# Long convolution by spectra: the signal's transform one pass ahead, the product of the spectra in four parts

## The chip, the cores and the metric

One core of one Trainium2 chip runs the whole program, in fp32. The metric is the device time of one execution in microseconds, the median of several.

## What is computed

The program is a chain of network blocks: an attention block, a Hyena block, two blocks with mixtures of experts. Only one stage of the Hyena block matters here, its long convolutions (`k_f` is the spectrum of a filter that a small network makes from the inputs, divided by the sum of its absolute values):

```python
def long_conv(u, k_f, skip):
    L = u.shape[1]
    y = jnp.fft.irfft(jnp.fft.rfft(uf, n=2 * L, axis=1) * k_f, n=2 * L, axis=1)[:, :L]
    return (y + uf * skip)
...
z = parts[0]
for o in range(HY_ORDER):                        # 2 orders
    z = parts[o + 1] * long_conv(z, k_f[:, o], skip[o])
```

L is 1024 and there are 1024 channels, so two orders of 1024 channels are convolved.

## The kernel before

`stage_long_conv` works in eight passes (PASSES), each of 256 channels (CCH) of one order; passes 0 to 3 are order 0, passes 4 to 7 order 1. Transforms are matmuls with constant matrices of cosines and sines, split by the token's remainder modulo four (PH = 4 phases, banks `x_bank0` to `x_bank3`) and two tiles of frequencies (MT = 2, index `ft`). One pass j needs, in the order of the data:

- **filters(j)**: TensorE makes eight filter tiles (matmul with `hid` and `w3`, L1861), and VectorE multiplies each with a decay into `filt` (L1998). The eight tiles share the four banks, so the second four wait until the first four are taken out.
- **sizes, totals, norm**: ScalarE takes absolute values into `mag` (two buffers, L1952), VectorE the maximum of the two halves into `total` (L2014), TensorE sums over partitions into `n_bank` (L1901). **tap(j)** on VectorE (L2022, L2024) adds the skip to the filter's first tap. `inverse_size` and `keep_size` (L2031, L2035) make `rnorm`, by which the result is scaled.
- **k_transform(j)**: 48 matmuls (96 records in the trace) on `filt`; ScalarE copies the banks to `xk` (L1958), VectorE's **k_butterfly** (L2042, L2043 and `turn`, L1819 to L1823) makes the spectrum `vk`.
- **the signal's transform**: 32 matmuls (64 records) on `u`; ScalarE copies to `xu`, then VectorE works on each `ft`: two sums and differences (L2067, L2068) and a `turn`; the product with `vk` (L2072 to L2074); its combination (L2075 to L2079); a second `turn` into `z` (L1819 to L1823). In the change these four parts are called enter, multiply, combine and leave.
- **back**: TensorE multiplies `z` with `inv` into two banks, one phase r after the other (16 records each, L1867 on `lc_y_bank`; here Y0 to Y3). VectorE scales each bank by `rnorm` into `y` (L2096; here y0 to y3), GpSimd multiplies `y` into `part` (L2113), and SP stores it.

`passes` runs a prologue, then a loop of six bodies (i = 0 to 5, `more` and `ahead` true), then body(6, more only) and body(7). Each engine runs its own instructions in order and waits on semaphores. Body i on TensorE before: signal i, k_transform(i + 1), the first four filter tiles of pass i + 2, then the wait for `z` of pass i, Y0, the second four tiles, Y1, Y2, norm(i + 2), Y3. VectorE: all parts of the product for both `ft`, the eight filter tiles of i + 2, then y0, two totals, y1, two totals, k_butterfly(i + 1, 0), y2, k_butterfly(i + 1, 1), tap(i + 2), y3, `rnorm` and size.

## Time and profile before

| | us |
|---|---|
| median of 3 runs | 4913.47 (4912.9 to 4920.15) |
| the profiled execution | 4910.12 |
| its span | 4908.1 |
| the long convolution in it | 1873.6 to 2453.8, about 580 |

The span is the time from the first to the last instruction. A row of the trace gives the start and the length in us of an instruction, or of several like ones in a row, its engine and line, the tiles it writes and reads, and how long its engine sat idle before it. PE is TensorE (its matmuls), PEld its weight loads, DVE VectorE, ACT ScalarE, POOL GpSimd. An fp32 matmul makes two records. Successive instructions of one engine overlap a little at their ends, so a chain is added up from start to start.

### The profile page before, as it was taken

The page shows a single profiled execution, that of the slowest core. Times are in us where ns is not written, and L with a number is a line of the kernel's source. Part 1 is how long each engine was busy: PE and PEld are TensorE (multiplying, and loading weights), DVE is VectorE, ACT ScalarE, POOL GpSimd, SP SyncE. Part 2 cuts the span into 40 slices and gives each one's busy share as a digit, 9 for nine tenths or more (in the row PEclk, how much of TensorE's full clock was granted, in tenths as well). Part 3 has the DMA queues.
Part 4 walks back from the last instruction along what each step waited for, and adds up shares of the span by engine and source line. Part 5 has one row for each costly group of instructions (what it writes and reads, how often), then busy time and mean ns, then how long its engine had stood idle before and what let it go on. Part 6 is the DMA issues. An engine that isn't in the chain of part 4 may idle for free. (4 is left out here: it accounts for less than half of the span.)

```text
span 4908.1 us, 59293 instructions
## 1 busy us (share of the span) xinstructions
PE 4173.6 (85%) x20947; PEld 2139.3 (44%) x20947; DVE 1898.4 (39%) x2965; ACT 1097.4 (22%) x1816; POOL 258.2 (5%) x366
## 2 busy tenths in 40 slices
PE   3699699998999998999679997786999599949995
PEld 0355355555444445777534444442333244413331
DVE  1233345443322113898734936532111333321112
ACT  0122255443110012222111135310000234100000
POOL 0000000000000000110100000000000200000001
PEclk7799899999999998999889999997999799969998
DMA  7322221112365511111161112135865511266666
GB/s 258 117 68 63 60 49 38 37 36 84 139 218 210 200 64 56 42 39 52 43 211 35 43 54 102 53 104 232 321 264 214 187 31 49 100 265 228 251 235 261
DMA packets 260939, 627.18 MB, mean 128 GB/s; under 512 B 73549, under 2 KB 153501, under 8 KB 240969
## 3 DMA queue, kind: packets, MB, share of 16 engines
q1 hardware_dynamic: 221906, 508.13, 29.3%
q0 software_dynamic: 19424, 94.01, 5.1%
q10 hardware_dynamic: 19480, 23.31, 1.3%
q8 instruction: 82, 1.34, 0.1%
q14 instruction: 47, 0.39, 0.0%
HBM read 1298.29 MB, written 113.53 MB: 288 GB/s over the span
## 5 line engine op out<-in xcount | busy, mean ns | idle before, releaser
L1645 PE MATMUL hyp_acc<-hy_hT,hyp_early_weights 128*128 128x512 f32 x768 | 335.9, 596 | 0.0
L3423 PE MATMUL blocks_h<-moe_w,blocks_xT 128*32 128x512 f32 x2560 | 291.1, 607 | 42.3 <-issue 42.3
L3423 PE MATMUL blocks_h<-od_hT,blocks_xT 128*32 128x512 f32 x1280 | 290.9, 608 | 25.7 <-DMA moe_w1b<-in_ex_w 20.6
L3444 PE MATMUL blocks_acc<-moe_w,blocks_hidT 128*32 128x512 f32 x2560 | 284.5, 596 | 11.2 <-DMA moe_w<-in_ex_w 9.9
L3423 PE MATMUL blocks_h<-moe_w1b,blocks_xT 128*32 128x512 f32 x1280 | 290.8, 608 | 0.0
L970 PE MATMUL att_scores<-att_kT,att_qT 64*128 64x512 f32 (+3 forms) x768 | 252.2, 549 | 22.7 <-DMA att_v<-scratch_V 22.7
L700 PE MATMUL lat_acc<-lat_w_in,lat_hT 128*128 128x512 f32 (+1 forms) x640 | 244.6, 538 | 2.2 <-DMA lat_w_in<-in_attn_w_in 2.2
L2209 PE MATMUL evp_acc<-ev_hT,evp_early_weights 128*128 128x512 f32 x512 | 224.6, 600 | 7.6 <-DVE evp_qkT L2350 5.6
L906 DVE TENSOR_REDUCE att_nmax<-att_scores 128x1 f32<-128x1280 f32 x128 | 190.2, 1486 | 102.2 <-PE att_scores L970 102.2
L994 PE MATMUL att_turn<-ident,att_probs 128*128 128x128 f32 x1280 | 192.5, 281 | 42.3 <-DVE att_o L936 22.5
L1645 PEld LDWEIGHTS hyp_acc<-hy_hT,hyp_early_weights 128*128 128x128 f32 x768 | 145.1, 191 | 174.3 <-issue 174.2
L874 ACT ACTIVATE att_probs<-att_scores,att_nmax 128x1280 f32<-128x1280 f32 x128 | 169.9, 1327 | 175.2 <-DVE att_nmax L906 172.4
L994 PEld LDWEIGHTS att_turn<-ident,att_probs 128*128 128x128 f32 x1280 | 143.0, 145 | 99.3 <-ACT att_probsT L885 43.8
L1867 PE MATMUL lc_y_bank<-lc_z,lc_inv 128*128 128x256 f32 x512 | 129.9, 416 | 63.5 <-DVE lc_z L1823 63.5
L3423 PEld LDWEIGHTS blocks_h<-moe_w,blocks_xT 128*32 128x32 f32 x2560 | 83.7, 112 | 220.2 <-issue 216.5
L885 ACT ACTIVATE att_probsT<-att_turn 128x512 f32<-128x512 f32 x256 | 139.2, 594 | 162.7 <-PE att_turn L994 162.2
L3423 PEld LDWEIGHTS blocks_h<-od_hT,blocks_xT 128*32 128x32 f32 x1280 | 76.6, 112 | 223.8 <-issue 223.8
L970 PEld LDWEIGHTS att_scores<-att_kT,att_qT 64*128 64x128 f32 (+1 forms) x768 | 113.1, 192 | 128.0 <-issue 127.9
L1867 PE MATMUL lc_x_bank<-lc_filt,lc_early_fwd 128*128 128x256 f32 x768 | 167.1, 379 | 1.3 <-issue 1.3
L700 PEld LDWEIGHTS lat_acc<-lat_w_in,lat_hT 128*128 128x128 f32 x640 | 114.6, 192 | 115.9 <-issue 115.6
L3444 PEld LDWEIGHTS blocks_acc<-moe_w,blocks_hidT 128*32 128x32 f32 x2560 | 79.7, 110 | 185.9 <-issue 180.0
L1004 PE MATMUL att_scores<-att_probsT,att_v 128*64 128x256 f32 x1280 | 152.3, 384 | 6.9 <-DVE att_probsT L915 6.1
(520 smaller groups left out, 6067.5 us busy)
## 6 DMA issues: line engine op xcount, KB each, us to landing
moe_w<-in_ex_w SPq DMA_DIRECT2D x320, 2048.0 KB
od_hT<-in_ex_w SPq DMA_DIRECT2D x80, 2048.0 KB
moe_w1b<-in_ex_w SPq DMA_DIRECT2D x80, 2048.0 KB
hyp_m_weights<-in_mod_w POOLq DMA_DIRECT2D x6, 8192.0 KB, 24.2
mod_weights<-in_ada_w SPq DMA_DIRECT2D x6, 4096.0 KB, 22.7
scratch_y_rows<-blocks_x ACTq DMA_DIRECT2D x40, 512.0 KB, 8.9
hyp_early_weights<-in_hy_w_in SPq DMA_DIRECT2D x8, 2048.0 KB
scratch_parts<-hyp_uT SPq DMA_DIRECT2D x24, 512.0 KB, 3.7
```

Of the source, the lines that this page charges most:

```text
L700: mm = nc.tensor.matmul(acc[:, (s * NCH + c) % 2, 0:b - a], hT[:, s, kt, :], w_in[:, kt, a:b], start=(kt == 0), stop=(kt == KT - 1))
L874: nc.scalar.activation(probs[:, j % 2, :], scores[:, j % 2, 0:KEYS], ACT.Exp, bias=nmax[:, j % 2:j % 2 + 1], accum_out=total[:, j % 2:j % ...
L885: nc.scalar.activation(probsT[:, c % 2, k:k + m, u * P:(u + 1) * P], turn[:, bank("probs", j, g), 0:m, :], ACT.Copy).then_inc(pT_act, 1)
L906: nc.vector.tensor_reduce(nmax[:, j % 2:j % 2 + 1], scores[:, j % 2, 0:KEYS], AX.X, ALU.max, negate=True).then_inc(maxed, 1)
L970: return nc.tensor.matmul(scores[:, b, a:z], qT[e, s, cols], kT[e, s, a:z], start=True, stop=True)
L994: last = nc.tensor.transpose(turn[:, bank("probs", j, g), a, :], probs[:, j % 2, (k + a) * P:(k + a + 1) * P], ident[:, :])
L1004: mm = nc.tensor.matmul(scores[e, 0, SPARE], v[:, 2 * c // TT, kt, :], probsT[:, c % 2, kt, :], start=(kt < 2), stop=(kt >= KTL - 2))
L1645: mm = nc.tensor.matmul(acc[:, m % 2, half * NC:(half + 1) * NC], weights[:, ws, kt, c:c + P], hT[:, kt, half * NC:(half + 1) * NC], start ...
L1867: mm = nc.tensor.matmul(out, m, x, start=(n == 0), stop=(n == len(terms) - 1))
L2209: mm = nc.tensor.matmul(out, lhs(kt), rhs(kt), start=(kt == 0), stop=(kt == KT - 1))
L3423: mm = nc.tensor.matmul(out[mine, :], xT[:, kt, mine], w[l][:, kt, :], start=(kt == 0), stop=(kt == KT - 1))
L3444: mm = nc.tensor.matmul(acc[mine, c, :], hidT[:, kt, mine], w2[l][:, kt, c * NC:(c + 1) * NC], start=(kt == 0), stop=(kt == FT - 1))
```

## The change

Pass i + 1's signal transform, `u_transform(i + 1)`, now stands in body i, behind k_transform(i + 1) and the first four filter tiles of i + 2. It writes the same four banks as the filter tiles, so TensorE first waits until VectorE has taken these four out (`tiles_gone`). The second four tiles come behind the signal's transform and ahead of Y0. The prologue gets the signal of pass 0, and the last body has no transform.

VectorE's product becomes `spectra(i, ft, parts)` with the four parts; `work` takes the place of the in-place `xu`, and `ktmp` lies in `tmp`. For `ft` 0 of pass i + 1, enter and multiply stand in body i between the two butterflies and the second four filter tiles, combine between y0 and y1, leave at the start of body i + 1. `ft` 1 is done whole in its own body. The two butterflies move from between y1 and y3 to ahead of the second four filter tiles, behind the first four. Where the filter work has ended (body 6), leave of `ft` 0 and enter of `ft` 1 of pass 7 stand between y1 and y3, the rest behind y3; body 7 has only the way back, and its product for pass 7 goes into `filt`. The skip is loaded by the pass, one small DMA each.

```diff
-        tmp, ktmp = sb("tmp", [P, PH, 2, CCH]), sb("ktmp", [P, 2, 2, CCH])
+        tmp, work = sb("tmp", [P, PH, 2, CCH]), sb("work", [P, PH, 2, CCH])
+        ktmp = tmp[:, 0:2, :, :]
...
-                sp.dma_start(skip[:, :], skips).then_inc(skip_in, 16)
+                def load_skip(j):
+                    sp.wait_ge(tapped, signals(j))
+                    sp.dma_start(skip[:, :], skips[:, bass.ds(j * CCH, CCH)]).then_inc(skip_in, 16)
...
+                load_skip(1)
...
+                    if ahead:
+                        load_skip(i + 2)
...
-                        if t < PH:
-                            if not isinstance(j, int) or j:
-                                pe.wait_ge(x_copied[b], signals(j * COPIES - MT))
-                        else:
+                        if not isinstance(j, int) or j:
+                            pe.wait_ge(x_copied[b], signals(j * COPIES - (MT if t < PH else 0)))
+                        if t >= PH:
                             pe.wait_ge(filt_ready, signals(j * NF + (t - PH + 1)))
...
+                def u_transform(j):
+                    pe.wait_ge(u_in, signals(j * 16 + 16))
+                    transform(u_parts, lambda ft: u_copied(j, ft) - 1, u_made)
+
+                def tiles_gone(j):
+                    for b in range(PH):
+                        pe.wait_ge(filt_ready, signals(j * NF + (b + 1)))
...
-                    filters(1, range(NF))
+                    filters(1, range(PH))
+                    tiles_gone(1)
+                    u_transform(0)
+                    filters(1, range(PH, NF))
                     norm(1)
                 def body(i, more, ahead):
                     if more:
                         pe.wait_ge(filt_ready, signals(i * NF + 2 * NF))
-                    pe.wait_ge(u_in, signals(i * 16 + 16))
-                    transform(u_parts, lambda ft: u_copied(i, ft) - 1, u_made)
-                    if more:
                         k_transform(i + 1)
                     if ahead:
                         filters(i + 2, range(PH))
+                        tiles_gone(i + 2)
+                    if more:
+                        u_transform(i + 1)
+                    if ahead:
+                        filters(i + 2, range(PH, NF))
                     pe.wait_ge(z_made, signals(i * MT + MT))
                     for r in range(PH):
-                        if ahead and r == 1:
-                            filters(i + 2, range(PH, NF))
                         if ahead and r == PH - 1:
                             norm(i + 2)
                         pe.wait_ge(y_scaled[r % 2], signals(i * (PH // 2) + r // 2))
...
                         for t in range(MT):
                             last = gather(y_bank[r % 2][:, t, :], [
-                                (inv[:, ft, r, cs, t * P:(t + 1) * P], z[:, ft, r, cs, :])
+                                (inv[:, ft, r, cs, t * P:(t + 1) * P], product_of(i)[:, ft, r, cs, :])
...
                 def copies(n, made, dst):
                     for ft in range(MT):
+                        if made is u_made and not (isinstance(n, int) and n == 0):
+                            act.wait_ge(xu_read, signals(n * MT + (ft + 1 - MT)))
...
                     decays(1)
+                    copies(0, u_made, xu)
...
-                    act.wait_ge(z_made, signals(i * MT))
-                    copies(i, u_made, xu)
                     if more:
                         k_copies(i + 1)
                     if ahead:
                         decays(i + 2)
+                    if more:
+                        copies(i + 1, u_made, xu)
+                    if ahead:
                         sizes(i + 2)
...
-                    dve.wait_ge(skip_in, signals(16))
-                    tt(extra[:, :], n_bank[0:1, 0:CCH], skip[:, bass.ds(j * CCH, CCH)], ALU.mult).then_inc(extra_made, 1)
+                    dve.wait_ge(skip_in, signals(j * 16 + 16))
+                    tt(extra[:, :], n_bank[0:1, 0:CCH], skip[:, :], ALU.mult).then_inc(extra_made, 1)
...
-                    dve.wait_ge(z_made, signals(j * MT))
+                    if not (isinstance(j, int) and j == 0):
+                        dve.wait_ge(z_made, signals((j - 1) * MT + (ft + 1)))
...
+                def spectra(i, ft, parts):
+
+
+                    links = Chain(dve, u_steps, i * (MT * U_STEPS) + ft * U_STEPS)
+                    x, k, w = xu[:, ft, :, :, :], vk[:, ft, :, :, :], work[:, :, :, :]
+
+                    def enter():
+                        dve.wait_ge(x_copied[PH - 1], signals(u_copied(i, ft)))
+                        dve.wait_ge(vk_ready, signals(i * MT + MT))
+                        dve.wait_ge(z_made, signals(i * MT + ft))
+                        tt(tmp[:, 0:2, :, :], x[:, 0:2, :, :], x[:, 2:4, :, :], ALU.add)
+                        tt(tmp[:, 2:4, :, :], x[:, 0:2, :, :], x[:, 2:4, :, :], ALU.subtract).then_inc(xu_read, 1)
+                        dve.wait_ge(xu_read, signals(i * MT + (ft + 1)))
+                        links.link(turn(nc.vector, tmp[:, 0, :, :], tmp[:, 1, :, :], tmp[:, 2, :, :], tmp[:, 3, :, :], w, 1))
+
+                    def multiply():
+                        links.n = 1
+                        links.link(tt(tmp[:, :, :, :], w, k, ALU.mult))
+                        tt(w[:, :, 0, :], w[:, :, 0, :], k[:, :, 1, :], ALU.mult)
+                        links.link(tt(w[:, :, 1, :], w[:, :, 1, :], k[:, :, 0, :], ALU.mult))
+
+                    def combine():
+                        links.n = 3
+                        links.link(tt(tmp[:, :, 0, :], tmp[:, :, 0, :], tmp[:, :, 1, :], ALU.subtract))
+                        links.link(tt(tmp[:, :, 1, :], w[:, :, 0, :], w[:, :, 1, :], ALU.add))
+                        tt(w[:, 0:2, :, :], tmp[:, 0:2, :, :], tmp[:, 2:4, :, :], ALU.add)
+                        links.link(tt(w[:, 2:4, :, :], tmp[:, 0:2, :, :], tmp[:, 2:4, :, :], ALU.subtract))
+
+                    def leave():
+                        if product_of(i) is z:
+                            dve.wait_ge(y_made, signals(i * PH))
+                        turn(nc.vector, w[:, 0, :, :], w[:, 1, :, :], w[:, 2, :, :], w[:, 3, :, :],
+                             product_of(i)[:, ft, :, :, :], 3).then_inc(z_made, 1)
+
+                    for part in parts:
+                        (enter, multiply, combine, leave)[part]()
...
-                    filters(1, range(NF))
+                    filters(1, range(PH))
+                    filters(1, range(PH, NF))
+                    spectra(0, 0, range(3))
                     totals(1, range(SUMS))
                     tap(1)
                     inverse_size(0)
...
                 def body(i, more, ahead):
-                    for ft in range(MT):
-                        link = Chain(dve, u_steps, i * (MT * U_STEPS) + ft * U_STEPS).link
-                        x, k = xu[:, ft, :, :, :], vk[:, ft, :, :, :]
-                        dve.wait_ge(x_copied[PH - 1], signals(u_copied(i, ft)))
-
-                        tt(tmp[:, 0:2, :, :], x[:, 0:2, :, :], x[:, 2:4, :, :], ALU.add)
-                        link(tt(tmp[:, 2:4, :, :], x[:, 0:2, :, :], x[:, 2:4, :, :], ALU.subtract))
-                        link(turn(nc.vector, tmp[:, 0, :, :], tmp[:, 1, :, :], tmp[:, 2, :, :], tmp[:, 3, :, :], x, 1))
...
-                        dve.wait_ge(vk_ready, signals(i * MT + (ft + 1)))
-                        link(tt(tmp[:, :, :, :], x, k, ALU.mult))
-                        tt(x[:, :, 0, :], x[:, :, 0, :], k[:, :, 1, :], ALU.mult)
...
-                        tt(x[:, 0:2, :, :], tmp[:, 0:2, :, :], tmp[:, 2:4, :, :], ALU.add)
-                        link(tt(x[:, 2:4, :, :], tmp[:, 0:2, :, :], tmp[:, 2:4, :, :], ALU.subtract))
-                        dve.wait_ge(y_made, signals(i * PH))
-                        turn(nc.vector, x[:, 0, :, :], x[:, 1, :, :], x[:, 2, :, :], x[:, 3, :, :], z[:, ft, :, :, :], 3)\
-                            .then_inc(z_made, 1)
+                    last = isinstance(i, int) and i == PASSES - 1
+                    if not last:
+                        spectra(i, 0, [3])
+                        spectra(i, 1, range(4))
                     if ahead:
                         filters(i + 2, range(PH))
+                    if more:
+                        for ft in range(MT):
+                            k_butterfly(i + 1, ft)
+                        spectra(i + 1, 0, range(2))
+                    if ahead:
                         filters(i + 2, range(PH, NF))
                     dve.wait_ge(rn_made, signals(i + 1))
                     for r in range(PH):
+                        if more and r == 1:
+                            spectra(i + 1, 0, [2])
+                        if more and not ahead:
+                            if r == 2:
+                                spectra(i + 1, 0, [3])
+                            if r == 3:
+                                spectra(i + 1, 1, [0])
                         if ahead and 0 < r <= 2:
                             totals(i + 2, range((r - 1) * PH // 2, r * PH // 2))
-                        if more and r >= PH - MT:
-                            k_butterfly(i + 1, r - (PH - MT))
                         if ahead and r == PH - 1:
                             tap(i + 2)
                         dve.wait_ge(y_made, signals(i * PH + (r + 1)))
                         dve.wait_ge(conv_done, signals(i * PH + max(r - 1, 0)))
                         tt(y[:, r % 2, :, :], y_bank[r % 2][:, :, :], rnorm[:, :].unsqueeze(1).to_broadcast([P, MT, CCH]),
                            ALU.mult).then_inc(y_scaled[r % 2], 1)
+                    if more and not ahead:
+                        spectra(i + 1, 1, range(1, 4))
                     if more:
                         inverse_size(i + 1)
                     if ahead:
```

The order in which TensorE's instructions stand, in the loop's body. Before (L1861 is a filter tile, L1867 every other matmul; counts are matmuls):

```order
L1867 MATMUL lc_x_bank<-lc_u,lc_early_fwd 128x256 x16
...
L1867 MATMUL lc_x_bank<-lc_filt,lc_early_fwd 128x256 x24
...
L1861 MATMUL lc_x_bank<-lc_early_w,lc_early_hid 128x512 x4
...
L1867 MATMUL lc_y_bank<-lc_z,lc_inv 128x256 x8
...
L1861 MATMUL lc_x_bank<-lc_early_w,lc_early_hid 128x512
...
L1867 MATMUL lc_n_bank<-lc_total,lc_early_ones 128x256 x8
L1867 MATMUL lc_y_bank<-lc_z,lc_inv 128x256 x8
```

and in the changed kernel (L1874 and L1880 are the same two lines):

```order
L1880 MATMUL lc_x_bank<-lc_filt,lc_early_fwd 128x256 x24
...
L1874 MATMUL lc_x_bank<-lc_early_w,lc_early_hid 128x512 x4
...
L1880 MATMUL lc_x_bank<-lc_u,lc_early_fwd 128x256 x16
...
L1874 MATMUL lc_x_bank<-lc_early_w,lc_early_hid 128x512 x4
...
L1880 MATMUL lc_y_bank<-lc_z,lc_inv 128x256 x16
...
L1880 MATMUL lc_n_bank<-lc_total,lc_early_ones 128x256 x8
L1880 MATMUL lc_y_bank<-lc_z,lc_inv 128x256 x8
```

The signal's matmuls moved from the head of the body to between the two groups of filter tiles, and nothing stands any more between Y0 and Y1.

VectorE around y0 and y1 in the loop's body. Before:

```order
L1998 TENSOR_TENSOR lc_filt<-lc_x_bank,lc_decay 128x512
...
L2096 TENSOR_TENSOR lc_y<-lc_y_bank,lc_rnorm 128x512
...
L2014 TENSOR_TENSOR lc_total<-lc_mag 128x512
...
L2042 TENSOR_TENSOR lc_ktmp<-lc_xk 128x512
L2043 TENSOR_TENSOR lc_ktmp<-lc_xk 128x512
```

and in the changed kernel (L2094 to L2096 are multiply, L2100 to L2103 combine, L2042 the totals, L2157 the y of one phase):

```order
L2094 TENSOR_TENSOR lc_tmp<-lc_work,lc_vk 128x2048
...
L2026 TENSOR_TENSOR lc_filt<-lc_x_bank,lc_decay 128x512
...
L2157 TENSOR_TENSOR lc_y<-lc_y_bank,lc_rnorm 128x512
L2100 TENSOR_TENSOR lc_tmp<-lc_tmp 128x4x256
...
L2101 TENSOR_TENSOR lc_tmp<-lc_work 128x4x256
...
L2102 TENSOR_TENSOR lc_work<-lc_tmp 128x1024
L2103 TENSOR_TENSOR lc_work<-lc_tmp 128x1024
...
L2042 TENSOR_TENSOR lc_total<-lc_mag 128x512
```

Four long instructions of the next pass's product now stand between y0 and the totals, and the butterflies that stood behind the totals are ahead of the second four filter tiles.

## Rows read from the trace of the kernel before

**Rows 1.** Who TensorE waited for, whole stage: sum, times, longest wait.

```profile
PE lc_y_bank L1867 <- DVE lc_z L1823: 63.5, 8, 28.4
```

**Rows 2.** One pass: stretch, length, busy PE, PEld, DVE, ACT, POOL, PEclk, DMA.

```profile
2072.80:2138.20 65.40, 60.82 (x259) 49.99 (x258) 59.34 (x83) 16.97 (x28) 6.82 (x4) 0.97 0.14 50
```

**Rows 3.** Timeline of TensorE in pass 1: start, length, engine, line, tiles, count.

```profile
2007.90 13.98 PE L1867 MATMUL lc_x_bank<-lc_u,lc_early_fwd 128*128 128x256 f32 x64
...
2021.71 20.88 PE L1867 MATMUL lc_x_bank<-lc_filt,lc_early_fwd 128*128 128x256 f32 x96
...
2042.43 3.60 PE L1861 MATMUL lc_x_bank<-lc_early_w,lc_early_hid 65*128 x8
...
2050.62 5.30 PE L1867 MATMUL lc_y_bank<-lc_z,lc_inv 128*128 128x256 f32 x16 [4.58 <-DVE lc_z L1823]
...
2066.10 3.62 PE L1867 MATMUL lc_n_bank<-lc_total,lc_early_ones 128*128 128x256 f32 x16
```

**Rows 4.** Timeline of VectorE, same pass: first instruction of each part of the product.

```profile
2015.64 1.22 DVE L2067 TENSOR_TENSOR lc_tmp<-lc_xu 128x1024 f32<-128x1024 f32 x1 [1.63 <-ACT lc_xu L1958]
...
2020.80 2.29 DVE L2072 TENSOR_TENSOR lc_tmp<-lc_xu,lc_vk 128x2048 f32<-128x2048 f32 x1
...
2025.52 1.23 DVE L2075 TENSOR_TENSOR lc_tmp<-lc_tmp 128x1024 f32<-128x1024 f32 x1
...
2030.52 0.69 DVE L1819 TENSOR_TENSOR lc_z<-lc_xu 128x512 f32<-128x512 f32 x1
...
2033.07 1.22 DVE L2067 TENSOR_TENSOR lc_tmp<-lc_xu 128x1024 f32<-128x1024 f32 x1
...
2050.41 0.68 DVE L1998 TENSOR_TENSOR lc_filt<-lc_x_bank,lc_decay 128x512 f32<-128x512 f32 x1
...
2051.98 1.87 DVE L1998 TENSOR_TENSOR lc_filt<-lc_x_bank,lc_decay 128x512 f32<-128x512 f32 x3
```

**Rows 5.** Timeline, same pass, from the totals behind y0: VectorE and GpSimd.

```profile
2060.60 2.37 DVE L2014 TENSOR_TENSOR lc_total<-lc_mag 128x512 f32<-128x512 f32 x2
...
2065.76 0.68 DVE L2042 TENSOR_TENSOR lc_ktmp<-lc_xk 128x512 f32<-128x512 f32 x1
...
2069.63 0.68 DVE L2096 TENSOR_TENSOR lc_y<-lc_y_bank,lc_rnorm 128x512 f32<-128x512 f32 x1
...
2070.39 2.25 POOL L2113 TENSOR_TENSOR lc_part<-lc_y,lc_part 128x512 f32<-128x512 f32 x1 [5.10 <-DVE lc_y L2096]
...
2071.55 1.65 DVE L1819 TENSOR_TENSOR lc_vk<-lc_ktmp,lc_xk 128x512 f32<-128x512 f32 x1
```

**Rows 6.** Timeline of VectorE, end of pass 0: y3, reciprocal, size.

```profile
2010.98 0.67 DVE L2096 TENSOR_TENSOR lc_y<-lc_y_bank,lc_rnorm 128x512 f32<-128x512 f32 x1
...
2011.79 1.75 DVE L2031 RECIPROCAL lc_rnorm<-lc_size 128x256 f32<-128x256 f32 x1
...
2013.58 0.42 DVE L2035 COPY lc_size<-lc_n_bank 128x256 f32<-128x256 f32 x1
```

**Rows 7.** Timeline of the stage's prologue: totals, norm, k_transform(0), second filter tiles of pass 1.

```profile
1888.29 1.28 DVE L2014 TENSOR_TENSOR lc_total<-lc_mag 128x512 f32<-128x512 f32 x2
...
1891.85 6.17 PE L1867 MATMUL lc_n_bank<-lc_total,lc_early_ones 128*128 128x256 f32 x16 [4.20 <-DVE lc_total L2014]
...
1899.28 20.96 PE L1867 MATMUL lc_x_bank<-lc_filt,lc_early_fwd 128*128 128x256 f32 x96 [1.26 <-issue]
...
1926.49 6.17 PE L1861 MATMUL lc_x_bank<-lc_early_w,lc_early_hid 65*128 65x512 f32 x8 [2.81 <-DVE lc_filt L2007]
```

**Rows 8.** Timeline of VectorE: y0 of passes 0, 6 and 7.

```profile
1994.89 0.68 DVE L2096 TENSOR_TENSOR lc_y<-lc_y_bank,lc_rnorm 128x512 f32<-128x512 f32 x1
...
2383.32 0.69 DVE L2096 TENSOR_TENSOR lc_y<-lc_y_bank,lc_rnorm 128x512 f32<-128x512 f32 x1 [5.82 <-issue]
...
2441.45 0.69 DVE L2096 TENSOR_TENSOR lc_y<-lc_y_bank,lc_rnorm 128x512 f32<-128x512 f32 x1 [5.72 <-issue]
```

**Rows 9.** DMA issues of the stage: tiles, queue, count, size, us to landing.

```profile
lc_u<-scratch_parts SPq DMA_DIRECT2D x8, 1024.0 KB, 4.8
```

More of the change, by code:

```diff
@@ L1760, in stage_long_conv @@
         inv = sb("inv", [P, MT, PH, 2, MT * P])
-        skip, skip_in = sb("skip", [1, PASSES * CCH]), sem("skip_in")
+        skip = sb("skip", [1, CCH])
         decay, mag = sb("decay", [P, TILES, CCH]), sb("mag", [P, 2, 2, 2, CCH])
@@ L1780, in stage_long_conv @@
                              "extra_made", "tapped"))
-        sized = sem("sized")
+        sized, skip_in, xu_read = sem("sized"), sem("skip_in"), sem("xu_read")
         u_steps, k_steps, vk_ready, z_made, y_made = (
@@ L1788, in stage_long_conv, with product_of @@
         COPIES = 2 * MT
-        U_STEPS = 7
+        U_STEPS = 6
         FIX = 2
         skips = d["hy_skip"].rearrange("a o c -> a (o c)")
+        z_last = filt[:, :, :, :].rearrange("p (m r) v c -> p m r v c", r=PH)
+        def product_of(i):
+            return z_last if isinstance(i, int) and i == PASSES - 1 else z
         def tokens(plane):
@@ L1833, in load_u @@
                     sp.dma_start(tiled(u), tokens(i)).then_inc(u_in, 16)
-                sp.dma_start(skip[:, :], skips).then_inc(skip_in, 16)
+                def load_skip(j):
+                    sp.wait_ge(tapped, signals(j))
+                    sp.dma_start(skip[:, :], skips[:, bass.ds(j * CCH, CCH)]).then_inc(skip_in, 16)
+                load_skip(0)
                 load_u(0)
@@ L2061, in body @@
                 def body(i, more, ahead):
-                    for ft in range(MT):
-                        link = Chain(dve, u_steps, i * (MT * U_STEPS) + ft * U_STEPS).link
-                        x, k = xu[:, ft, :, :, :], vk[:, ft, :, :, :]
-                        dve.wait_ge(x_copied[PH - 1], signals(u_copied(i, ft)))
-                        tt(tmp[:, 0:2, :, :], x[:, 0:2, :, :], x[:, 2:4, :, :], ALU.add)
-                        link(tt(tmp[:, 2:4, :, :], x[:, 0:2, :, :], x[:, 2:4, :, :], ALU.subtract))
-                        link(turn(nc.vector, tmp[:, 0, :, :], tmp[:, 1, :, :], tmp[:, 2, :, :], tmp[:, 3, :, :], x, 1))
-                        dve.wait_ge(vk_ready, signals(i * MT + (ft + 1)))
-                        link(tt(tmp[:, :, :, :], x, k, ALU.mult))
-                        tt(x[:, :, 0, :], x[:, :, 0, :], k[:, :, 1, :], ALU.mult)
-                        link(tt(x[:, :, 1, :], x[:, :, 1, :], k[:, :, 0, :], ALU.mult))
-                        link(tt(tmp[:, :, 0, :], tmp[:, :, 0, :], tmp[:, :, 1, :], ALU.subtract))
-                        link(tt(tmp[:, :, 1, :], x[:, :, 0, :], x[:, :, 1, :], ALU.add))
-                        tt(x[:, 0:2, :, :], tmp[:, 0:2, :, :], tmp[:, 2:4, :, :], ALU.add)
-                        link(tt(x[:, 2:4, :, :], tmp[:, 0:2, :, :], tmp[:, 2:4, :, :], ALU.subtract))
-                        dve.wait_ge(y_made, signals(i * PH))
-                        turn(nc.vector, x[:, 0, :, :], x[:, 1, :, :], x[:, 2, :, :], x[:, 3, :, :], z[:, ft, :, :, :], 3)\
-                            .then_inc(z_made, 1)
+                    last = isinstance(i, int) and i == PASSES - 1
+                    if not last:
+                        spectra(i, 0, [3])
+                        spectra(i, 1, range(4))
                     if ahead:
                         filters(i + 2, range(PH))
+                    if more:
[3 more added lines that the diff above has]
+                    if ahead:
                         filters(i + 2, range(PH, NF))
```

## The prediction

> **What bounds the kernel now.** The change lies in one stage, so I read only that. First, who waited for whom: in the whole stage TensorE waited for data only for the product `z` on VectorE, 63.5 us in eight waits, the longest 28.4 [rows 1]. Second, one pass: of 65.4 us TensorE is busy 60.8, VectorE 59.3, the granted clock is 0.97 of full [rows 2]. Two engines are nearly full; the reader should see that emptying one wait soon meets the other. Third, TensorE's timeline [rows 3]. A full-speed record takes 20.72 / 96 = 0.216 us (start of the 96 records at 2021.71 to the next row). So a pass needs 13.8 (signal, 64) + 20.7 (filter spectrum, 96) + 2 x 3.4 (filter tiles) + 4 x 3.45 (Y0 to Y3) + 3.45 (norm) = 58.6 us. The rest of 65.4 is one stall of about 5 us in front of Y0 and its sequel: Y0 takes 5.30 where 16 like records take 3.62, because the PE clock, granted 2.4 GHz before, is at 1.2 GHz after the stall.
>
> **What the change removes.** The product `z` of a pass is now finished about 20 us into the body, while TensorE still has 38 us of transforms to do. The wait in front of Y0 goes: at most 65.4 - 58.6 = 6.8 us a pass. At the end of the stage there is more: between y0 of pass 6 and y0 of pass 7 lie 58.1 us [rows 8], most of it the whole product of pass 7 with TensorE idle.
>
> **The VectorE chain.** I cut VectorE's work by starts [rows 4]: enter 2015.64 to 2020.80 = 5.16; multiply 4.72; combine 5.00; leave 2.55; all four 17.43. Four filter tiles with the first-tap repair 2050.41 to 2053.85 = 3.44, so four further ones 4 x 0.61 = 2.44. A butterfly 2065.76 to 2069.63 = 3.87 [rows 5]. y3 to the reciprocal 0.81, then 1.79, then the copy's 0.4: 3.0 [rows 6]. A y takes 0.61 to the next start. Two totals take 1.28 alone [rows 7] but 2.37 behind a y [rows 5]: GpSimd's multiply starts then. Behind y2 it is a `turn` instruction that takes 1.65 where 0.69 is usual, while GpSimd's takes 2.25. So each y that is followed by work on VectorE costs about 1.05 more.
>
> The page "SBUF — State Buffer" of the Trainium skill (section "Who interferes with whom") says that a VectorE instruction with two SBUF inputs and a GpSimd instruction that reads SBUF exclude each other, the later one waiting to the end. The trace agrees in kind; taken literally, with GpSimd's undisturbed length for the hold, it would make each case some 0.2 us dearer. The rule speaks against this change, since combine is such work. The sum uses the 1.05 of the rows.
>
> **A pass of the loop, from y0.** y0 0.6, combine 5.0 + 1.05, two totals 1.2, y1 0.6, a wait of 0.4 for ScalarE's second absolute value, two totals 1.2 + 1.05: 11.1 us until the last total. Only then may norm run; Y2 was done long before, 6.9 us behind Y0. So a new stall of about 4 us stands in front of norm. It resembles the removed one (5 us), so I give it a like sequel. Its bounds are the 1.7 that Y0 lost in the shown pass [rows 3] and the 2.55 that a norm lost in the prologue (6.17 against 3.62) [rows 7, 3], below them nothing; I take 2.0, near the loop's own row. Norm 3.45, Y3 3.45, 2.0, handovers 0.4: y3 starts at 20.4, Y3 ended at 20.2, and there TensorE starts the next filter spectrum.
>
> From y3 VectorE goes 3.0 + leave 2.55 + the whole `ft` 1, 17.43, + four filter tiles 3.44 = 26.4. TensorE has done 20.7 + 3.4 = 24.1 by then and stands at `tiles_gone` until 26.6 after its start: a second stall of 2.5 us behind filter tiles. The nearest row is the prologue's 2.81 us stall, also behind four filter tiles: the eight records behind it take 6.17 where 3.60 is usual [rows 7, 3], so the clock was down. I charge 1.5 (ends: 0 and 2.6). Then the signal 13.8 + 1.5 to 42.0, filter tiles to 45.4, Y0 to 49.1. VectorE is at 26.6 + two butterflies 7.7 + enter and multiply 9.9 + four tiles 2.4 = 46.7, and waits for Y0. From y0 to y0: 20.2 + 49.1 = **69.3 us**.
>
> **The last passes.** Pass 5 to 6 has no filter work in its second half and VectorE carries it: 20.4 + 3.0 + 2.55 + 17.43 + 7.74 + 9.88 = 61.0. Before, the six intervals from y0 of pass 0 to y0 of pass 6 took 2383.32 - 1994.89 = 388.4 [rows 8]. Now 5 x 69.3 + 61.0 = 407.5: **+19.1**. Pass 6 to 7: four y 2.4, combine 5.0, leave 2.55, enter 5.16, then multiply, combine and leave 12.3, four GpSimd holds 4.2, together 31.6, then Y0 of pass 7 at 1.2 GHz 5.6 (3.62 + 2.0) and handovers: 37.4 instead of 58.1: **-20.7**. Behind y0 of pass 7 nothing changes.
>
> **The prologue pays for the pass that is ahead.** Up to k_transform(0), which starts at 1899.28 and lasts 20.7 [rows 7], nothing changes. Its filter tiles come out of the banks at about 1928.3 (the second ones could start at 1926.49 on the first being out, three more at 0.61). TensorE has then stood for 5 us, so signal 0 runs 13.8 + 2.0 to 1944.2; second filter tiles out at 1948.3; enter, multiply, combine 14.9 to 1963.2; totals 3.6 and norm with tap 7.4 (1888.29 to 1891.85 to 1899.28) to 1974.2, the start of k_transform(1). By the scheme above, here without the first tail, y0 of pass 0 comes 48.1 later: 2022.3 against 1994.89: **+27.4**.
>
> What costs nothing: `tmp` shared with the butterflies, since VectorE runs both in order. The signal's load is issued behind the store and the reload of `part` on SP; three transfers of 1 MB at 4.8 each [rows 9] are 14.4 us, and the data is wanted 26.7 us into the body. The skip loads wait for a tap of the pass before and hold SP for nothing; the small row is wanted 60 us later. The other bound, if SP came late, would be a stall as long as it is late; no row suggests it.
>
> **Sum.** 27.4 + 19.1 - 20.7 = +25.8 us. On the profiled execution's 4910.12 that is 4935.9; that execution lies 3.35 below the median of 4913.47, so for the median I forecast **4939 us**. About 0.2% (10 us) is what this kernel's measurement can tell from no change.
>
> **Rivals.** (a) *The clock stays up.* The stalls are shorter than the removed one, and a stall of 4 us between full matmuls has no row here. Then an interval is 65.8, the six take 5 x 65.8 + 59.0 = 388.0, and the prologue 25.9, the tail -20.7: +4.8, or about 4918. The intermediate, one stall with a cold sequel, gives 5 x 1.5 to 2.0 more, 4926 to 4929, and still counts as mine. (b) *It ends faster: GpSimd does not hold combine.* Place: behind y0 and y1, in front of norm. If combine and the totals run undisturbed, the stall before norm shrinks from 4 to 2 us, an interval is 63.7 with the clock up, the six take 5 x 63.7 + 57 = 375.5, the last 33: 25.9 - 12.9 - 25 = -12, 4901. It decides from an interval of about 63.5 to 64 on: there the eight passes balance the prologue. For it: an interval below 64 leaves 5 us of idle or slow TensorE, which the old one had too. Against it: three of four y in the old trace show the hold. (c) *Worse:* both stalls leave TensorE slow for longer, as the upper bounds of 2.6 each allow, and the loop's back edge on VectorE, hidden by a wait before, becomes visible: 2 to 3 us a pass, 4950 to 4955. (d) *It does not do what it says:* `z` still late. Excluded nearly: its last part is 23 us into a body in which Y0 cannot start before 41.
>
> **Chances.** Mine with the intermediate 0.58 (4925 to 4948), (c) 0.16, (a) 0.15, (b) 0.09, (d) 0.02. Faster by over 0.2%: 0.08; within 0.2%: 0.13; slower: 0.79. For 8 in 10 the range takes in (a)'s time and (c)'s: 4913 to 4958.
>
> **What the changed profile would show.** TensorE's wait for `z` only once with weight, at pass 7, some 20 us; new waits for `lc_total` of about 4 us before norm and for `lc_filt` of 2.5 us before the signal; y0 of pass 0 near 2022; intervals near 69; the last one near 37; instructions behind y0 and y1 longer by 1. My forecast is wrong if intervals are under 66, if the granted clock in the loop is not below the old 0.97, or if the first y0 comes before 2015.

## The result, and the profile after

The changed kernel takes 4947.35 us against 4914.01 us before (medians of four runs each): a ratio of 1.0066, 95% interval 1.0046 to 1.0085. It is slower, as forecast, and 4947 lies inside the range of 4913 to 4958; the forecast was 4939. A second series, beside other kernels below, gave 1.0054 (1.0042 to 1.0066), 26.9 us.

The profiled execution took 4957.55 us, 47.4 more than the profiled one of before. Of that, 2.8 us lie ahead of the long convolution (it starts at 1876.43, not 1873.65), 31.1 in it (609.2 us from the first filter matmul to the start of the last y, before 578.1), and 13.5 behind it, where nothing was changed. In the second series' profile the stage is 605.8 us, 27.7 longer than before, about the 26.9 measured there, and the rest of that execution is 6.0 us longer than in the profiled one of before. So only the stage is explained here.

TensorE in a pass of the loop of the changed kernel, to be held against [rows 3] (start, length, engine, line, tiles, count, idle before it and its releaser):

```profile
2137.23 3.60 PE L1874 MATMUL lc_x_bank<-lc_early_w,lc_early_hid 65*128 x8
2143.40 15.48 PE L1880 MATMUL lc_x_bank<-lc_u,lc_early_fwd 128*128 128x256 f32 x64 [2.57 <-DVE lc_filt L2026]
2158.72 3.60 PE L1874 MATMUL lc_x_bank<-lc_early_w,lc_early_hid 65*128 x8
2162.15 10.53 PE L1880 MATMUL lc_y_bank<-lc_z,lc_inv 128*128 128x256 f32 x48
2176.68 5.41 PE L1880 MATMUL lc_n_bank<-lc_total,lc_early_ones 128*128 128x256 f32 x16 [4.00 <-DVE lc_total L2042]
2181.92 3.62 PE L1880 MATMUL lc_y_bank<-lc_z,lc_inv 128*128 128x256 f32 x16
```

The stall in front of Y0 is gone, and Y0 to Y2 run through at full speed. Two stalls stand in its place: 2.57 us until VectorE has taken the filter tiles out, and 4.00 us until the last total. Behind each, TensorE is slow: the signal's transform takes 15.48 where it took 13.98, norm 5.41 where it took 3.62. The next pass is worse in both:

```profile
2212.26 3.35 PE L1880 MATMUL lc_x_bank<-lc_u,lc_early_fwd 128*128 128x256 f32 x7 [2.57 <-DVE lc_filt L2026]
...
2228.97 3.60 PE L1874 MATMUL lc_x_bank<-lc_early_w,lc_early_hid 65*128 x8
...
2246.93 6.25 PE L1880 MATMUL lc_n_bank<-lc_total,lc_early_ones 128*128 128x256 f32 x16 [3.99 <-DVE lc_total L2042]
```

There the signal lasts from 2212.26 to 2228.97, and norm 6.25. Who waited for whom in the stage (engine and line, what it waited for, sum, times, longest), against [rows 1]:

```profile
PE lc_n_bank L1880 <- DVE lc_total L2042: 47.1, 8, 18.9
PE lc_y_bank L1880 <- DVE lc_filt L1830: 20.3, 1, 20.3
PE lc_x_bank L1880 <- DVE lc_filt L2026: 19.2, 7, 4.9
```

The 63.5 us of waits for the product have become 20.3, and TensorE's waits for totals and tiles, 11.2 us before and all of them in the prologue, have become 66.3. VectorE and GpSimd behind y0 of pass 0, against [rows 5]:

```profile
2025.81 0.69 DVE L2157 TENSOR_TENSOR lc_y<-lc_y_bank,lc_rnorm 128x512 f32<-128x512 f32 x1 [0.75 <-PE lc_y_bank L1880]
2026.42 1.22 DVE L2100 TENSOR_TENSOR lc_tmp<-lc_tmp 128x1024 f32<-128x1024 f32 x1
2026.59 2.17 POOL L2176 TENSOR_TENSOR lc_part<-lc_y,lc_part 128x512 f32<-128x512 f32 x1 [259.39 <-DVE lc_y L2157]
2027.67 2.17 DVE L2101 TENSOR_TENSOR lc_tmp<-lc_work 128x1024 f32<-128x1024 f32 x1
...
2035.21 1.42 DVE L2042 TENSOR_TENSOR lc_total<-lc_mag 128x512 f32<-128x512 f32 x1 [0.25 <-ACT lc_mag L1976]
```

Combine fills the time between y0 and the totals; one of its four instructions takes 2.17 where its neighbours take 1.22, and the last total (1.42 where 0.69 is usual) ends at 2036.63, just before norm starts at 2036.68.

### The profile page after: what moved, and what is told of

Same layout as the page of the kernel before. It is cut to its first block and busy times, and to the rows that moved or that the text cites. A ratio compares the mean times of both kernels' runs of the same rounds, so it can differ in the third digit from the quotient of the medians.

```text
span 4955.5 us, 59312 instructions
## 1 busy us (share of the span) xinstructions
PE 4199.7 (85%) x20947; PEld 2152.3 (43%) x20947; DVE 1892.9 (38%) x2965; ACT 1094.2 (22%) x1816; POOL 258.3 (5%) x366
## 5 line engine op out<-in xcount | busy, mean ns | idle before, releaser
L3486 PE MATMUL blocks_h<-od_hT,blocks_xT 128*32 128x512 f32 x1280 | 289.5, 606 | 27.3 <-DMA moe_w1b<-in_ex_w 22.2
L3507 PE MATMUL blocks_acc<-moe_w,blocks_hidT 128*32 128x512 f32 x2560 | 285.4, 598 | 11.2 <-DMA moe_w<-in_ex_w 9.8
L1880 PE MATMUL lc_x_bank<-lc_filt,lc_early_fwd 128*128 128x256 f32 x768 | 167.2, 379 | 2.6 <-DVE lc_filt L2052 1.3
L3372 DVE TENSOR_TENSOR blocks_hid<-blocks_hid,blocks_h 128x512 f32<-128x512 f32 x40 | 27.5, 688 | 337.1 <-PE blocks_h L3486 330.8
```

Of the source, the lines that this page charges most:

```text
L1880: mm = nc.tensor.matmul(out, m, x, start=(n == 0), stop=(n == len(terms) - 1))
L3486: mm = nc.tensor.matmul(out[mine, :], xT[:, kt, mine], w[l][:, kt, :], start=(kt == 0), stop=(kt == KT - 1))
L3507: mm = nc.tensor.matmul(acc[mine, c, :], hidT[:, kt, mine], w2[l][:, kt, c * NC:(c + 1) * NC], start=(kt == 0), stop=(kt == FT - 1))
```

## Experiments

The profiles of all variants are read in the same two ways: the interval from y0 of one pass to y0 of the next (before 65.5 on average over the first five, in the changed kernel 70.0), and the time from the stage's first filter matmul to y0 of pass 0 (before 121.2, changed 149.4). Three of the variants were run once: the second filler alone and the two with GpSimd made small. Of these only the long convolution in the profile is read.

**The changed kernel again.** No edit.

> The changed kernel once more, beside the kernel before, to place the difference: its long convolution took 31 us longer in the profile (568 us before, 599 after, first filter matmul to y0 of pass 7), while the whole profiled execution was 47 us longer. If the stage is all of it, the ratio is about 1.0063 (+31 us); if the rest belongs to the change too, 1.0095.

4944.07 against 4917.19 us, ratio 1.0054 (1.0042 to 1.0066). Intervals 68.9, then 70.3, 69.7, 70.3, 69.7; first y0 at 148.5, last interval 37.1. Outside the stage this execution is 6.0 us longer than the profiled one of before, where the first was 16.3 longer; since the median difference is 26.9 and the stage's 27.7, I take both for scatter between executions.

**Combine behind y2.**

```diff
-                        if more and r == 1:
+                        if more and r == (PH - 1 if ahead else 1):
                             spectra(i + 1, 0, [2])
```

> One edit of the changed kernel: in the loop, combine of the next pass stands behind y2 and ahead of the tap, not between y0 and y1, so that the totals that norm waits for come about 6 us earlier. Theory (VectorE's work between y0 and the last total sets norm's start): the 4.0 us stall in front of norm is gone, and with it the cold norm. From y0: last total at 6.1, Y2 ends at 6.9, norm and Y3 to 13.8, the tap behind combine at 15.0; the rest of the chain 49.1. Interval about 64 instead of 70.0 us; the kernel about 35 us faster than the changed one, some 5 us faster than before. Rival (VectorE is simply full, whatever the order): combine costs the same anywhere, the interval stays at 69 to 70.

4906.87 us, ratio to before 0.9975 (0.9965 to 0.9985), 37 us faster than the changed kernel in the same series. Timeline of this variant from y0 on:

```profile
2085.28 0.69 DVE L2157 TENSOR_TENSOR lc_y<-lc_y_bank,lc_rnorm 128x512 f32<-128x512 f32 x1 [0.74 <-PE lc_y_bank L1880]
...
2091.99 3.62 PE L1880 MATMUL lc_n_bank<-lc_total,lc_early_ones 128*128 128x256 f32 x16
...
2100.18 20.98 PE L1880 MATMUL lc_x_bank<-lc_filt,lc_early_fwd 128*128 128x256 f32 x96 [1.12 <-DVE lc_filt L2052]
...
2126.65 14.08 PE L1880 MATMUL lc_x_bank<-lc_u,lc_early_fwd 128*128 128x256 f32 x64 [2.05 <-DVE lc_filt L2026]
```

Norm starts with no idle time and takes 3.62. The tap is now 1.1 us late for the next filter spectrum, and the stall for the tiles stays; here no slow signal follows, in the passes next to it one does:

```profile
2189.01 15.76 PE L1880 MATMUL lc_x_bank<-lc_u,lc_early_fwd 128*128 128x256 f32 x64 [2.06 <-DVE lc_filt L2026]
```

With that, intervals alternate between 62.37 and 64.05, 63.4 on average, against 64 forecast; the kernel gained a little more than the 35 us expected, and lies 10 us below the kernel before, not 5. The rival (VectorE full, whatever the order) is out: the same instructions in another place are worth 6.6 us a pass.

**Fillers in both stalls, and in one.** The matmuls go to a bank nobody reads; `keep_busy(n)` issues n of them (two records each):

```diff
                         filters(i + 2, range(PH))
+                        keep_busy(5)
                         tiles_gone(i + 2)
...
                         if ahead and r == PH - 1:
+                            keep_busy(8)
                             norm(i + 2)
```

> The changed kernel with matmuls into an unused bank that nobody reads, in the loop only: five in front of the wait for the filter tiles (2.2 us) and eight in front of norm (3.5 us); the data they wait for comes no sooner. Theory (part of each interval is TensorE at 1.2 GHz behind the two stalls): the signal's transform takes 13.98 instead of 15.5 to 16.9, norm 3.62 instead of 5.4 to 6.3, the interval falls from 70.0 to about 66.5, the kernel by 18 to 20 us. Rival (the slow records are hidden behind VectorE): records get faster, the interval stays at 69 to 70.

4920.92 us, ratio to before 1.0006 (0.9997 to 1.0015), 23 us faster than the changed kernel. TensorE of this variant (L1926 is the filler):

```profile
2097.20 3.62 PE L1926 MATMUL lc_spare<-lc_inv,lc_early_ones 128*128 128x256 f32 x16
2101.36 3.72 PE L1880 MATMUL lc_n_bank<-lc_total,lc_early_ones 128*128 128x256 f32 x16 [0.55 <-DVE lc_total L2048]
...
2132.53 2.32 PE L1926 MATMUL lc_spare<-lc_inv,lc_early_ones 128*128 128x256 f32 x10
2135.28 14.08 PE L1880 MATMUL lc_x_bank<-lc_u,lc_early_fwd 128*128 128x256 f32 x64 [0.43 <-DVE lc_filt L2032]
```

The waits end when they ended before, but what follows is at full speed: the granted clock is 1.00 in every interval, where the changed kernel has 0.93. The interval is 65.8 in every pass (about 66.5 was expected): 4.2 us of the changed kernel's 70.0 are TensorE at 1.2 GHz. With the second filler alone (in front of norm):

> The changed kernel with matmuls into an unused bank in front of norm only (eight, 3.5 us), none in front of the signal's transform. With both filled the interval was 65.8 against 70.0 us. Theory (each stall leaves slow records behind it that lie on the chain): norm takes 3.7 instead of 5.4 to 6.3, the signal's transform stays at 15.5 to 16.9, the interval is 67.5 to 68.2, so that the two stalls share the 4.2 about evenly. Rival (only one of them counts, since VectorE hides the other): 65.8 or 70.

```profile
2098.91 3.72 PE L1880 MATMUL lc_n_bank<-lc_total,lc_early_ones 128*128 128x256 f32 x16 [0.55 <-DVE lc_total L2047]
...
2132.83 16.70 PE L1880 MATMUL lc_x_bank<-lc_u,lc_early_fwd 128*128 128x256 f32 x64 [2.59 <-DVE lc_filt L2031]
```

Intervals of 67.5 and four times 68.3 to 68.4, 68.2 on average; the one execution took 4929.34 us, 4917.7 for the kernel before beside it. So about 1.8 us of the 4.2 hang on the stall in front of norm and 2.4 on the shorter stall behind the filter tiles.

**The kernel before with a filler.** Ten matmuls in front of its wait for `z`:

```diff
+                    if ahead:
+                        keep_busy(10)
                     pe.wait_ge(z_made, signals(i * MT + MT))
```

> The kernel before the change, with ten matmuls into an unused bank (4.3 us) in front of its wait for z in the loop; z comes no sooner. Theory (of the 6.8 us that the stall costs, 1.5 to 3 are the 1.2 GHz behind it): Y0 takes 3.62 instead of 5.1 to 6.8, the interval falls from 65.5 to 63.3 to 63.6, six passes give 11 to 13 us, ratio 0.9975. Rival (the clock falls whatever fills the gap, or what follows is bound by VectorE): 65.5, no change.

4906.79 us, ratio 0.9978 (0.9968 to 0.9988). Its TensorE, against [rows 3]:

```profile
2108.09 4.48 PE L1905 MATMUL lc_spare<-lc_inv,lc_early_ones 128*128 128x256 f32 x20
2112.84 3.72 PE L1867 MATMUL lc_y_bank<-lc_z,lc_inv 128*128 128x256 f32 x16 [0.26 <-DVE lc_z L1823]
```

The interval is 63.51 in all five, 1.95 less, with the product no earlier. The granted clock is 1.00 in all five, against 0.95 to 0.97 before. Useless matmuls gained 10 us where the large change lost about 30.

**GpSimd made small.** It multiplies 8 of the 256 channels (`r, 0:8` in place of `r, :`).

> The changed kernel with GpSimd multiplying only 8 of the 256 channels behind each y, so that it holds SBUF for a moment instead of 1.3 us; the output is not the reference's, and the later stages get other data, so only the long convolution is read. Theory (GpSimd's multiply holds the VectorE instruction behind each y by about 1.0 us): combine and the totals lose the two long instructions, the stall in front of norm falls from 4.0 to about 2 us, the interval from 70.0 to 66 to 68, depending on whether the clock still falls. Rival (the two long instructions are long by themselves): nothing moves.

```profile
2089.65 1.22 DVE L2100 TENSOR_TENSOR lc_tmp<-lc_tmp 128x1024 f32<-128x1024 f32 x1
2089.81 1.13 POOL L2176 TENSOR_TENSOR lc_part<-lc_y,lc_part 128x16 f32<-128x16 f32 x1 [50.54 <-DVE lc_y L2157]
2090.90 1.23 DVE L2101 TENSOR_TENSOR lc_tmp<-lc_work 128x1024 f32<-128x1024 f32 x1
...
2098.24 5.41 PE L1880 MATMUL lc_n_bank<-lc_total,lc_early_ones 128*128 128x256 f32 x16 [2.33 <-DVE lc_total L2042]
```

The instruction that took 2.17 takes 1.23, the stall in front of norm is 2.33 instead of 4.00, and the intervals are 67.2 and four times 68.3 to 68.6: 68.1 on average, 1.9 us less than 70.0. The hold is real and its price is as forecast; but a stall of 2.33 us still leaves norm at 5.3 to 5.4 in four of the five intervals (in the first, norm took 3.72 behind the same stall), and the gain is just short of the 2 to 4 us that I expected.

**The prologue's product later.**

```diff
-                    spectra(0, 0, range(3))
                     totals(1, range(SUMS))
                     tap(1)
+                    spectra(0, 0, range(3))
```

> The changed kernel with the prologue's product of pass 0 (enter, multiply, combine: 14.9 us) behind tap(1), not in front of the totals of pass 1, so that norm(1) and k_transform(1) start about 15 us earlier. Theory (the prologue's 27 us are VectorE work that only stands earlier, and VectorE is the bound until y0 of pass 0): norm's wait shrinks from 18.9 to about 4 us, but the first y0 stays within 2 us of 148.5 us behind the start, and the kernel's time within 0.1% of the changed kernel's. Rival (norm held back by the product is the cost): the first y0 comes some 13 us earlier, the kernel is 13 us faster.

4948.59 us, ratio to before 1.0062 (1.0047 to 1.0077). Its TensorE from norm(1) on:

```profile
1953.43 6.30 PE L1880 MATMUL lc_n_bank<-lc_total,lc_early_ones 128*128 128x256 f32 x16 [4.20 <-DVE lc_total L2042]
1961.05 20.98 PE L1880 MATMUL lc_x_bank<-lc_filt,lc_early_fwd 128*128 128x256 f32 x96 [1.31 <-DVE lc_filt L2052]
...
2001.21 16.66 PE L1880 MATMUL lc_x_bank<-lc_u,lc_early_fwd 128*128 128x256 f32 x64 [15.75 <-DVE lc_filt L2026]
```

Norm's wait fell from 18.9 to 4.2 us, and the wait for the tiles of pass 2 grew from 1.38 to 15.75. The first y0 comes at 151.2: no earlier, and 2.7 behind the 148.5, where 2 was allowed. The product's place makes no gain, because from the second four filter tiles of pass 1 to the first y0 (78 us) VectorE idles only about 11 us in either order, 6 to 7 of them behind norm. Ahead of these tiles it does wait, 17 to 18.5 us, behind TensorE's stall of 4.9 us and signal 0. So that part of the prologue is TensorE's, and the next variant shortens it.

**Signal first.** TensorE does the signal's transform ahead of all filter tiles; the first four tiles come ahead of Y0, the second four between Y0 and Y1, as in the kernel before; VectorE takes all eight behind multiply. The core of it:

```diff
-                        filters(i + 2, range(PH))
-                        tiles_gone(i + 2)
                     if more:
                         u_transform(i + 1)
                     if ahead:
-                        filters(i + 2, range(PH, NF))
+                        filters(i + 2, range(PH))
...
+                        if ahead and r == 1:
+                            filters(i + 2, range(PH, NF))
```

> The changed kernel with the filter tiles back behind the signal's transform: TensorE runs k_transform, signal, four tiles, Y0, four tiles, Y1, Y2, norm, Y3, with no wait for tiles to be gone; VectorE takes all eight tiles behind enter and multiply. Combine stays between y0 and y1. Theory (the stall for the tiles costs 2.6 us and a slow signal of 1.5 to 2.9, but the stall in front of norm stays, set by VectorE): the signal's transform takes 13.98, the interval 67 to 68 instead of 70, the prologue 6 to 7 us less; the kernel 15 to 20 us faster than the changed one, still slower than before by 5 to 12. Rival (the two stalls are in series on TensorE alone): the interval falls by the full 4.5 us, to 65.5.

4930.55 us, ratio to before 1.0026 (1.0016 to 1.0035); intervals 68.3 (67 to 68 expected), first y0 at 140.6, 8 to 9 us earlier (6 to 7 expected).

```profile
2077.75 3.70 PE L1874 MATMUL lc_x_bank<-lc_early_w,lc_early_hid 65*128 x8 [1.63 <-DVE lc_filt L2032]
...
2092.95 6.57 PE L1880 MATMUL lc_n_bank<-lc_total,lc_early_ones 128*128 128x256 f32 x16 [4.59 <-DVE lc_total L2039]
...
2123.53 13.98 PE L1880 MATMUL lc_x_bank<-lc_u,lc_early_fwd 128*128 128x256 f32 x64
```

The stall for the tiles and the slow signal are gone, about 5 us a pass, but only 1.7 reach the interval (a little less than the 2 to 3 expected): a stall of 1.63 us has come in front of the second filter tiles, which wait until VectorE has taken the first tile out, the stall in front of norm has grown from 4.00 to 4.59 and VectorE sets it, and norm behind it takes 6.57.

**Both edits.**

> Both edits at once: filter tiles behind the signal's transform, and combine behind y2. Theory: TensorE has no stall above 2 us left in the loop; the chain is VectorE's own work, about 61 us of starts with three holds by GpSimd: interval 61.5 to 62.5, against 63.4 with combine alone; the first y0 6 us earlier. The kernel 12 to 16 us faster than with combine alone, about 4893, a ratio to before of 0.995. Rival (with combine late, TensorE's remaining 58.6 us and its clock bound the pass): 63, no gain over combine alone.

4889.23 us, ratio to before 0.9940 (0.9926 to 0.9953): 28 us faster than the kernel before, 55 to 58 faster than the changed one (its two medians), and a little faster than the 4893 expected. Busy time and granted clock (the third number from the end of each row) over one interval, first this version, then the changed kernel, in the order of columns of [rows 2]:

```profile
2072.10:2133.51 61.41, 59.20 (x258) 48.46 (x257) 59.02 (x82) 16.74 (x28) 6.75 (x4) 1.00 0.15 53
```

```profile
2096.09:2165.81 69.72, 63.15 (x257) 51.32 (x256) 57.75 (x82) 16.63 (x28) 6.36 (x4) 0.93 0.12 47
```

Every interval is 61.4 us, TensorE's clock is at its full level throughout, and both engines are near 59 us busy. TensorE's stalls are two of 1.1 us, in front of the second filter tiles and in front of the filter spectrum.

**Both edits, GpSimd small.**

> The version with signal first and combine late, with GpSimd multiplying only 8 of the 256 channels; the output is not the reference's and the later stages get other data, so only the long convolution is read. Theory (that version's 61.4 us are VectorE's chain, three instructions of it held about 1.0 us each by GpSimd): the interval falls to 58.6 to 59.3, where TensorE's own 58.6 us take over. Rival (something else bounds the 61.4): it stays within 0.5 us.

Intervals 60.6, 61.9, 62.6, 60.6, 60.6: a miss. The three undisturbed ones gained 0.8, not 2 or more; the other two are longer than the version's own 61.4. TensorE around the border between the second and the third interval, and VectorE's y0:

```profile
2126.73 5.04 PE L1874 MATMUL lc_x_bank<-lc_early_w,lc_early_hid 65*128 x8 [1.21 <-DVE lc_filt L2032]
2131.56 9.16 PE L1880 MATMUL lc_y_bank<-lc_z,lc_inv 128*128 128x256 f32 x32
...
2132.41 0.68 DVE L2153 TENSOR_TENSOR lc_y<-lc_y_bank,lc_rnorm 128x512 f32<-128x512 f32 x1
```

and TensorE, then VectorE's y1 and y2, one pass later:

```profile
2190.69 3.70 PE L1874 MATMUL lc_x_bank<-lc_early_w,lc_early_hid 65*128 x8 [1.21 <-DVE lc_filt L2032]
2194.22 7.07 PE L1880 MATMUL lc_y_bank<-lc_z,lc_inv 128*128 128x256 f32 x32
...
2197.88 0.69 DVE L2153 TENSOR_TENSOR lc_y<-lc_y_bank,lc_rnorm 128x512 f32<-128x512 f32 x1 [0.94 <-PE lc_y_bank L1880]
...
2201.33 0.69 DVE L2153 TENSOR_TENSOR lc_y<-lc_y_bank,lc_rnorm 128x512 f32<-128x512 f32 x1 [1.54 <-PE lc_y_bank L1880]
```

The second filter tiles wait 1.2 us for the first one to be taken out, in every pass. Behind one of these five stalls the clock was down once, and y0 falls into that stretch: the tiles take 5.04 in place of 3.70, which lengthens the second interval by 1.3 us, Y1 and Y2 take 9.16 in place of 7.07, which lengthens the third by 2.0. In the undisturbed passes VectorE, no longer held, waits 0.94 us for Y1 and 1.54 for Y2. So from y0 to y2 nothing is gained (6.30 us, 6.31 with GpSimd whole), and only the hold in combine, behind y2, counts: y2 to y3 takes 6.91 in place of 7.76. The 61.4 are not VectorE's alone; TensorE sets the way from y0 to y2, with its stall of 1.2 us, which the forecast of 58.6 left out.

## Why the prediction was right, and where it was off

**Direction and mechanism.** The product ahead of its use did remove the wait in front of Y0, and the gain went into two new waits: the totals behind combine, and the filter tiles behind the product. Moving combine alone turned the loss into a gain of 10 us, which shows the first; signal first removed the second.

**The chain from y0 to norm.** Forecast 11.1 us and a stall of about 4; measured 10.87 (2025.81 to 2036.68, where norm starts) and 4.00. The held instructions behind y0 and y1 are there: 2.17 and 1.42, and the small GpSimd shows that GpSimd holds them. The stall for the tiles: 2.5 forecast, 2.57 measured. The wait of y0 for Y0, 2.4 forecast from the numbers of the sum, was 0.74 only, because VectorE arrived later than my sum let it: in the loop, enter waits for ScalarE's copies of the slow signal, 1.5 or 2.9 us in turn, a wait that my sum did not have.

```profile
2152.64 1.23 DVE L2087 TENSOR_TENSOR lc_tmp<-lc_xu 128x1024 f32<-128x1024 f32 x1 [1.50 <-ACT lc_xu L1984]
```

**The interval** was 70.0, not 69.3. The mis-sized terms are the two of the clock. For the slow signal I took 1.5 out of 0 to 2.6; it lost 1.5 or 2.9 in turn, 2.3 on average. For norm 2.0; it lost 1.8 or 2.6, 2.2 on average. Their sum is 1.0 more than the 3.5 that I charged, the shorter chain gives 0.2 back. The prologue row of a stall behind filter tiles, 6.17 against 3.60 [rows 7, 3], was the right neighbour, and its full 2.6 the better value.

**The other terms.** Prologue +27.4, measured +28.1 and +27.3 in the two profiles, and the first y0 did not move forward with the place of the product. Its last part, 48.1 us from k_transform(1) to y0, stands in the prediction without its working; it measured 48.3 and 46.8. From pass 6 to 7 -20.7, measured 58.13 to 37.44, -20.7, and -21.0 in the second profile. Six intervals +19.1, measured +23.6 and +21.4. Together +25.8 forecast, +31.1 and +27.7 in the profiles; the medians differ by 33.3 (interval 23 to 42) and 26.9. So the sum is 1 us low against the second difference and 8 against the first, and what it had too small is the loop, by 4.5 us in the first profile and 2.3 in the second.

**The rivals.** (a), the clock stays up: out, and priced, since that is what the fillers made: 65.8 us an interval as I had worked out, and 3.7 us above the kernel before, where I had 4.8. (b), GpSimd does not hold combine: out. Removing the hold did not make the kernel faster than before either: the intervals stayed at 68.1 on average where (b) has 63.7 with the clock up, because a stall of 2.33 us was, but for the first pass, still enough for a slow norm, and the stall for the tiles stood as before. (c) holds in part: the clock's share was near my upper bound for the signal, but the back edge on VectorE stayed hidden, since y3 still waited 2.23 us for Y3. (d): the product is in time.

The page "SBUF — State Buffer" of the Trainium skill (section "Who interferes with whom") has the later of two such instructions wait for the other's end. The rows agree, though both instructions grew: each was the later one once. GpSimd's started at 2026.59, while VectorE's of 2026.42 ran until 2027.64, and lasted until 2028.76 (2.17 in place of 1.26); VectorE's next started at 2027.67 and ended 1.1 us behind GpSimd's, at 2029.84 (2.17 in place of 1.22). With GpSimd made small its instruction, which takes 0.22 undisturbed, still took 1.13 behind the same VectorE instruction, ended at 2090.94, and VectorE's next was 1.23. What VectorE lost was 0.95, so the rows' 1.05 was a better charge than GpSimd's whole 1.26.

## What to carry to other kernels

When two engines are both nearly full, moving work ahead pays only if it does not stand between a short chain and its consumer: look at what the other engine's next small operation waits for, and put long independent work behind it, not in front. In this stage a stall of TensorE of 2.3 to 5 us cost its length and then, all but once in the loops, 1.5 to 3.2 us more of half-speed matmuls behind it, so that two short stalls cost more than one long one: 4.2 us a pass against 1.95. Work out the first and the last pass by themselves; here a pipeline one pass deeper won 21 us at the end and paid 27 at the start.

## What the runs showed of the hardware

A filler of matmuls into an unused bank, ended by the same wait, kept the clock up in all five loop intervals of each of the two kernels that had one in every long stall, and was worth 2 us a pass for a stall of 5 and 4.2 for two stalls of 2.6 and 4.

At the stage's start, behind 4.8 us without work, 16 records of filter tiles follow one another at the 1.2 GHz level to the end: 13.82 us (granted clock 0.50 from 1880 to 1890), where 8 of them take 3.60 in the loop. They did so in all twelve profiles (13.7 to 14.0 us).

```profile
1876.43 13.82 PE L1874 MATMUL lc_x_bank<-lc_early_w,lc_early_hid 65*128 65x512 f32 x16 [4.81 <-PEq L83]
```

Around filter tiles even short stalls can leave the engine slow: 2.57 us did in every pass of the changed kernel's loop, 2.05 us did in every second pass of the variant with combine behind y2 (15.76 and 14.08), and 1.2 us once in five passes of the last variant. The 1.63 us of signal first and the 1.1 us of both edits never did. The same stall of 1.38 us in the prologue of the changed kernel left the signal slow in the first profile and not in the second:

```profile
2003.35 15.53 PE L1880 MATMUL lc_x_bank<-lc_u,lc_early_fwd 128*128 128x256 f32 x64 [1.38 <-DVE lc_filt L2026]
```

```profile
2000.09 14.08 PE L1880 MATMUL lc_x_bank<-lc_u,lc_early_fwd 128*128 128x256 f32 x64 [1.38 <-DVE lc_filt L2026]
```

So the length of the stall alone does not decide; what does stays open.
